# The score products of two attention heads issued in alternation, after both value transposes

## What is computed

```python
def moba_core(q, q_pos, means, fetch_k, fetch_v):
    ...
    scale = HEAD_DIM ** -0.5
    ...
    s_own = jnp.einsum('hqd,hqtd->hqt', q, k_own).astype(jnp.float32) * scale
    s_own = jnp.where(own_pos <= q_pos[:, None], s_own, NEG_INF)
    p = jax.nn.softmax(jnp.concatenate([s_sel, s_own], axis=-1), axis=-1).astype(v_own.dtype)
    ...
    return (jnp.einsum('hqjt,hqjtd->hqd', p_sel, v_sel)
            + jnp.einsum('hqt,hqtd->hqd', p_own, v_own))
```

## Time and profile before

| | us |
|---|---|
| median of 3 runs | 1263.07 (1261.01 to 1264.86) |
| the profiled execution, its own time | 1262.67 |
| its span, first to last instruction | 1260.5 |
| TensorE busy | 1223.6 (97%) |
| VectorE busy | 780.0 (62%) |
| ScalarE busy | 571.3 (45%) |
| GpSimd busy | 750.9 (60%) |
| the eight pairs, about 75 to 242 in the trace | some 21 each |

### The profile page before, as it was taken

One profiled execution on the slowest core, in us unless ns is written; L12 is line 12 of the kernel. 1 busy time (PEld: TensorE's weight loads), 2 busy tenths in 40 slices (PEclk: granted clock), 3 DMA queues, 4 the chain that ended last, 5 costly groups with the idle time before them and its releaser, 6 DMA issues.

```text
span 1260.5 us, 23698 instructions
## 1 busy us (share of the span) xinstructions
PE 1223.6 (97%) x7517; PEld 1057.1 (84%) x7517; DVE 780.0 (62%) x1737; ACT 571.3 (45%) x1287; POOL 750.9 (60%) x622
## 2 busy tenths in 40 slices
PE   7999999999898999999999999999999999999997
PEld 4877888754797999999999999999888888888756
DVE  3679787643304999900189999995454456665433
ACT  3322223340333455556555555444555555555535
POOL 0048250000571669998866666666677688788635
PEclk8999999998898999999999999999999999999999
DMA  5465575375463446666645544455566688788633
GB/s 186 158 219 155 175 243 156 109 248 195 141 184 119 142 130 199 189 185 178 195 137 143 143 142 143 138 143 149 169 188 191 191 286 273 235 285 279 192 91 111
DMA packets 99863, 224.88 MB, mean 178 GB/s; under 512 B 11682, under 2 KB 12306, under 8 KB 99274
## 3 DMA queue, kind: packets, MB, share of 16 engines
q1 hardware_dynamic: 96762, 214.52, 55.3%
q0 software_dynamic: 2304, 8.39, 1.9%
q10 hardware_dynamic: 720, 1.01, 0.3%
HBM read 215.61 MB, written 8.19 MB: 178 GB/s over the span
## 4 chain that ended last, share of the span: by engine, by line
PE 67%; issue 1%; DVE 1%; ACT 1%; POOL 0%; DVEq 0%; POOLq 0%; ACTq 0%
PE bank L1480 29%; PE bank L1510 28%; PE bank L1490 5%; PE bank L1433 2%; PE bank L1541 1%; PE bank L1445 1%; PE bank L1457 1%; PE bank L1530 0%; PE bank L1403 0%; ACT hl L1600 0%; POOL hl L1371 0%; DVE acts L1741 0%; DVE acts L1891 0%; ACT acts L1706 0%; POOL hl L1356 0%
## 5 line engine op out<-in xcount | busy, mean ns | idle before, releaser
L1356 POOL TENSOR_TENSOR hl<-ring,hl 128x512 fp32r<-128x512 f32 x448 | 586.6, 1320 | 194.5 <-ACT hl L1590 187.5
L1590 ACT CAST hl<-ring 128x512 fp32r<-128x512 f32 x512 | 317.1, 620 | 301.0 <-PE bank L1510 170.0
L1480 PE MATMUL bank<-split,hl 128*128 128x256 f32 x3072 | 378.4, 282 | 0.4 <-ACT hl L1590 0.3
L1480 PEld LDWEIGHTS bank<-split,hl 128*128 128x128 f32 x3072 | 366.2, 188 | 0.8 <-issue 0.5
L1510 PE MATMUL bank<-hl,split 128*128 128x512 f32 x1524 | 353.6, 394 | 0.0
L1510 PEld LDWEIGHTS bank<-hl,split 128*128 128x128 f32 x1524 | 285.9, 188 | 67.7 <-issue 0.9
L472 PE MATMUL pj<-xn,ring 128*128 128x264 f32 x704 | 165.0, 391 | 1.6 <-DMA ring<-in_w_ring 1.6
L1861 DVE TENSOR_TENSOR split<-acts,split 128x256 fp32r<-128x256 f32 x128 | 129.5, 1037 | 50.0 <-ACT split L1682 46.6
L472 PEld LDWEIGHTS pj<-xn,ring 128*128 128x128 f32 x704 | 132.2, 192 | 26.0 <-issue 2.8
L1868 DVE TENSOR_TENSOR hl<-ring,hl 128x512 fp32r<-128x512 f32 x64 | 46.8, 732 | 117.0 <-ACT hl L1590 117.0
L448 POOL TENSOR_TENSOR wo<-ring,wo 128x512 fp32r<-128x512 f32 x32 | 43.5, 1369 | 123.3 <-ACT wo L835 123.2
(11 more groups left out here) (319 smaller groups left out, 1245.8 us busy)
## 6 DMA issues: line engine op xcount, KB each, us to landing
ring<-in_uv SPq DMA_DIRECT2D x256, 256.0 KB, 2.7
ring<-in_v_rows SPq DMA_DIRECT2D x256, 256.0 KB, 3.1
ring<-in_w_ring SPq DMA_DIRECT2D x76, 512.0 KB, 3.7
room<-in_cache_k SPq DMA_DIRECT2D x16, 512.0 KB, 4.8
room<-in_cache_v SPq DMA_DIRECT2D x16, 512.0 KB, 4.5
hs<-in_state_ssm SPq DMA_DIRECT2D x8, 512.0 KB, 4.5
out_ssm_s<-hs SPq DMA_DIRECT2D x8, 512.0 KB, 5.7
acts<-x_rows SPq DMA_DIRECT2D x8, 512.0 KB, 5.1
```

Of the source, the lines that this page charges most:

```text
L1356: nc.gpsimd.tensor_tensor(hl[:, r % HL, 1], raw[:, r], hl[:, r % HL, 0].bitcast(F32), ALU.subtract).then_inc(lo_done, 1)
L1480: mm = nc.tensor.matmul(out, hl[:, r % HL, m, k * P:(k + 1) * P], split[:, x, kk, 0:TP], start=(kk == 0 and n == 0), stop=(kk == KD - 1 an ...
L1590: nc.scalar.copy(hl[:, r % HL, 0], raw[:, r]).then_inc(hi_done, 1)
```

## The change

In `scores(c)` the six calls of a pair are put into another order. Before: transpose, narrow product, wide product of head 0, then the same three of head 1. After: the two transposes, the two narrow products, the two wide products, head 0 ahead of head 1 each time. Operands, output columns, waits ahead of the block and the two increments of `s_ready` (behind each head's wide product) are the same.

```diff
                     for j in range(2):
-                        r = slice(j * HD, (j + 1) * HD)
                         nc.tensor.transpose(hd[j][:, 3 * P:4 * P], proj[:, V0 + c, j * P:(j + 1) * P], ident)
-                        nc.tensor.matmul(hd[j][:, 0:P], proj[r, Q0 + c, 0:P], proj[r, K0 + c, 0:P], start=True, stop=True)
-                        nc.tensor.matmul(hd[j][:, P:3 * P], proj[r, Q0 + c, P:TP], proj[r, K0 + c, 0:TP], start=True, stop=True
-                                         ).then_inc(s_ready, 1)
+                    for q0, q1, k1, at in ((0, P, P, 0), (P, TP, TP, P)):
+                        for j in range(2):
+                            r = slice(j * HD, (j + 1) * HD)
+                            mm = nc.tensor.matmul(hd[j][:, at:at + k1], proj[r, Q0 + c, q0:q1], proj[r, K0 + c, 0:k1], start=True, stop=True)
+                            if q0:
+                                mm.then_inc(s_ready, 1)
```

## The result

The changed kernel took 1254.22 us (median of 10 runs, 1250.89 to 1256.52) against 1261.87 for the kernel before (10 runs). The mean of the changed kernel over its two series is 1255.8 us (22 runs). That of the kernel before is 1261.2 in the 48 runs of the second and third series, whose clocks are on record. All 69 runs of the kernel before would make it 5.0; the two series in which both kernels ran give 7.2 and 3.7, further apart than such an error allows, so the size of the gain is known to some 2 us only.

A forecast was written before the change was run, and what follows sets the result against it. TensorE was taken to bound the kernel, with VectorE's chain ending six pairs; 6 x 0.23 + 2 x 0.57 = 2.5 us, so 1263.07 - 2.5 gives 1260.6 us, range 1257.6 to 1265.0.

The forecast's parts named there:

- TensorE bounds, but six pairs end in VectorE's chain: In the eight pairs: TensorE busy 159.4 of 164.0 us, but pairs 0 to 5 gain only what VectorE gains.
- TensorE after, one behind another: 1.82: First transpose to next tile, products without overlap: 1.82 us in place of 2.17, gain 0.35 a pair.
- Overlap of the heads: Products of the two heads side by side three times: 0 to 0.44 us a pair, 0.22 taken.
- The weight loads go one by one: In the block, narrow passes can't move closer than 0.11 us; only one pair of wide passes overlaps.
- VectorE gains 0.23: VectorE's second mask addition starts 2.04 us behind the first transpose in place of 2.27, 0.23 earlier.
- full overlap: All three neighbours of the heads overlap, loads too: 0.79 us on TensorE, 0.45 on VectorE, 1258.8 us; chance 0.22.
- No order could give more than the 0.51: VectorE's gain per pair is capped by its wait of 0.51 us for head 1's wide product.
- The sum: Over the eight pairs: 6 x 0.23 + 2 x 0.57 = 2.5 us gained.
- The gain reaches the end: Behind the pairs, the other engines start from TensorE, so the 2.5 us pass on whole.
- The slower rival: Moving between partition halves stops the stream like a shape change: 0.22 us longer a pair, 1264.9 us; chance 0.08.
- The likeliest case: Products in the block one by one or with only the wide overlap, 1261.0 to 1260.6 us; chance 0.57.

The follow-up runs named there:

- the heads in turn: Against the kernel before, only the transposes moved together; each head keeps its narrow and wide product side by side: 1255.04 us, ratio 0.9952.
- the second series: The changed kernel measured again without an edit, against the kernel before: 1258.01 us (12 runs), ratio 0.9982.
- the first series: First measurement of the changed kernel against the kernel before: 1254.22 us against 1261.87 (10 runs each), ratio 0.9943.

## Why the prediction was wrong, point by point

- *TensorE bounds, but six pairs end in VectorE's chain.* Right in kind. The waits for L745 and L1060 grew in those pairs, by 3.0 us in all (3.9 to 6.9; 1.8 were forecast), and with the chain shortened every pair but the first gained the whole block.
- *TensorE after, one behind another: 1.82.* The parts hold. The two shape changes were worth 0.35, and the transposes are 0.11 apart.
- *Overlap of the heads: 0.22, from none to 0.44.* **This step failed**, the bound as much as the choice. It let only three neighbours run side by side, since it took the order of calls as the order of starts. All four passes of head 1 run under head 0's, so both of its terms in the sum, 0.22 and 0.44, go to nothing: 0.65 measured. With the heads in turn they do so too, four passes out of order. The Trainium skill, "TensorE: Matmul & The Clock Gate", section "Part 3: Packing small matmuls — row/col tiling", gives starts some 4 ns apart. The trace has 7 ns, and 13 with the heads in turn. The same section of the Trainium skill has the products start and end in strict order of the program. The kernel with the heads in turn speaks against that, since its block is the same 1.17.
- *The weight loads go one by one.* Wrong, and it was the reason for the choice. That no row showed two loads side by side was no evidence, since no two neighbours in the kernel before used different halves of the rows. Now two loads start 7 ns apart.
- *VectorE gains 0.23.* It gained 0.53. The wide product of head 0 starts at 0.64, the value of the full overlap. The second addition starts 0.47 behind the first, not 0.56: the duration of a record was taken for the distance of starts, which the same text knew to be different on TensorE. "No order could give more than the 0.51" fell for the same reason.
- *The sum.* With the measured terms, 6 x 0.53 + 2 x 0.99 = 5.2 us. That this is so near to the 5.3 of the means is in part luck, for the traces show 4.2 for the pairs: the two pairs without VectorE gained their 1.0 each, but the six others 2.2 together and not 3.2. The steps from pair 3 and pair 4 gained 0.0 in the first traces, where GpSimd's L438 holds the end of L979, and 0.5 and 0.3 in the second; the step from pair 0 gained 0.8. This term was missing. The distance from 4.2 to 5.3 is about what the clock's average explains (1.3).
- *From 1260.6 to 1254.22.* Of these 6.4 us, 1.2 are the starting point (1263.07 was the median of three runs, ten gave 1261.87) and 2.7 the terms above. The other 2.5 are no term of the sum: in the second series the two medians are 2.7 us apart, in the first 7.7. With its terms as measured the forecast would have been 1257.9.
- *The gain reaches the end.* Right: nothing behind the pairs took it back. The start of the first key page moved by 1.0 more than the first transpose of the last pair, as the block says.
- *The slower rival.* No load stands late between the heads, so the halves don't count as different shapes. The Trainium skill, "TensorEngine Tiling (Array Packing)", section "Key Properties", has the engine drain at a change of the mode and not at one of the tile alone. This trace agrees: the only late loads of the block are those of its two shape changes, 0.17 and 0.33.
- *The likeliest case was the wrong one of those told.* Full overlap stood there with 1258.8 and a chance of 0.22, and was itself 0.2 short on TensorE and 0.08 on VectorE.

What stays open: why the first series shows 7.2 us and the second 3.7, of which the granted clock explains a part; whether the engine takes up head 1 as soon as its rows are free or by a rule on the passes, and how far ahead it looks. Four passes was the most tried. Open too is why the stretches at half clock fell where they did.

## What to carry to other kernels

Products that contract over 64 rows and use different halves of the partitions (and different PSUM banks) cost half (eight passes in the 0.93 us of four) if nothing of another shape stands between them, so gather the transposes ahead of them and count the shape changes; their exact order matters less. Before costing a shorter block, look at who ends TensorE's waits in the stretch: here six of eight pairs ended in a chain of VectorE, and moving three of its instructions into its own idle time was worth nearly twice the change. And a VectorE instruction that runs beside GpSimd's can take almost three times as long (0.75 us against 0.28 in L979), so an earlier start may only meet more of that.

## What was not expected of the hardware

- Passes of the second head start 7 ns behind those of the first (13 ns with the heads in turn), out of the order of the program, with their weight loads side by side; eight passes took the 0.93 us of four.
- Two VectorE additions of 128 x 384 that wait for nothing start 0.47 us apart, though each record lasts 0.56.
- VectorE's L979 (128 x 128) takes 0.28 us alone and 0.75 while GpSimd's L438 runs.
- The same kernel's runs lie up to 12.6 us apart (before: 1254.6 to 1267.2 in one series), along the mean granted clock, at 1.1 us for each 0.001.
